# RWKV chunk matrices as 64x64 blocks, four heads to a stream, with the second stream half a round behind

## The reference

```python
def step(S, inp):
    rt, wt, kt, vt, kkt, at = inp
    sa = einsum('bhvk,bhk->bhv', S, -kkt)
    S = S * wt[:, :, None, :] + sa[..., None] * (kkt * at)[:, :, None, :] + vt[..., None] * kt[:, :, None, :]
    return S, einsum('bhvk,bhk->bhv', S, rt)
S1, y = lax.scan(step, S0, xs)      # 512 steps
```

## Time and profile before

| | |
|---|---|
| timed, median of 3 runs | 5242.58 us (5240.49 to 5243.71) |
| profiled execution | 5239.91 us, span 5238.2 us |
| TensorE busy | 91% of the span |
| VectorE / ScalarE / GpSimd busy | 55% / 30% / 26% |
| mean granted TensorE clock | 0.937 |

### The profile page before, as it was taken

One profiled execution on the slowest core, in us unless ns is written; L12 is line 12 of the kernel. 1 busy time (PEld: TensorE's weight loads), 2 busy tenths in 40 slices (PEclk: granted clock), 3 DMA queues, 4 the chain that ended last, 5 costly groups with the idle time before them and its releaser, 6 DMA issues. The chain is left out here.

```text
span 5238.2 us, 59995 instructions
## 1 busy us (share of the span) xinstructions
PE 4753.3 (91%) x23383; PEld 3839.2 (73%) x23383; DVE 2866.4 (55%) x4356; ACT 1594.0 (30%) x3108; POOL 1339.3 (26%) x571
## 2 busy tenths in 40 slices
PE   8996649699999999999997987789999999999997
PEld 5665328577888887788886655577788787788886
DVE  1044455424987862566663016813977872566665
ACT  1020202112456662222222012311366563222222
POOL 0000000001443444444441000001433444444442
PEclk9995759899999999999998996889999999999999
DMA  4232100022566685555552231132566676455552
GB/s 148 81 105 68 36 17 1 34 87 87 160 178 174 194 237 173 188 194 194 194 193 77 94 97 49 37 105 75 155 178 183 176 220 207 163 193 193 194 193 91
DMA packets 531708, 709.99 MB, mean 136 GB/s; under 512 B 47625, under 2 KB 415874, under 8 KB 510434
## 3 DMA queue, kind: packets, MB, share of 16 engines
q1 hardware_dynamic: 526004, 689.08, 40.8%
q0 software_dynamic: 4608, 16.78, 1.0%
q10 hardware_dynamic: 814, 0.29, 0.0%
HBM read 552.62 MB, written 149.21 MB: 134 GB/s over the span
## 5 line engine op out<-in xcount | busy, mean ns | idle before, releaser
L2304 PE MATMUL ps<-h_parts,u_parts 128*128 128x512 f32 x6144 | 1431.1, 393 | 23.2 <-PEq L1803 13.3
L2555 PE MATMUL ps<-w_parts,v_parts 128*128 128x512 f32 x6144 | 1398.1, 390 | 14.8 <-DVE w_parts L2540 14.8
L2555 PEld LDWEIGHTS ps<-w_parts,v_parts 128*128 128x128 f32 x6144 | 1156.8, 188 | 256.0 <-POOL v_parts L2526 15.5
L2304 PEld LDWEIGHTS ps<-h_parts,u_parts 128*128 128x128 f32 x6144 | 1151.5, 189 | 260.6 <-POOL u_parts L1781 13.8
L1781 POOL TENSOR_TENSOR u_parts<-u_turned,u_parts 128x1024 fp32r<-128x1024 f32 x256 | 664.1, 2595 | 2065.0 <-ACT u_parts L1776 2064.9
L2540 DVE TENSOR_TENSOR w_parts<-w_rows,w_parts 128x512 fp32r<-128x512 f32 x256 | 625.1, 2442 | 481.5 <-ACT w_parts L2519 481.5
L211 PE MATMUL ps<-h,arena 128*128 128x264 f32 (+2 forms) x2176 | 486.3, 387 | 81.3 <-DMA arena<-in_even_w_out_dram 33.4
L2526 POOL TENSOR_TENSOR v_parts<-u_rows,v_parts 128x1024 fp32r<-128x1024 f32 x172 | 413.0, 2402 | 539.9 <-ACT v_parts L2517 539.9
L211 PEld LDWEIGHTS ps<-h,arena 128*128 128x128 f32 (+1 forms) x2176 | 411.6, 189 | 156.6 <-DMA arena<-in_even_w_out_dram 33.8
L2082 DVE TENSOR_TENSOR onehots<-iota,choice 128x1024 f32<-128x1024 f32 x256 | 385.6, 1546 | 189.4 <-PE ps L2336 187.8
L1768 DVE STREAM_TRANSPOSE u_turned<-u_rows 128x1024 f32<-128x1024 f32 x256 | 317.0, 1238 | 234.1 <-POOL u_parts L1781 212.4
(11 more groups left out here) (487 smaller groups left out, 4258.5 us busy)
## 6 DMA issues: line engine op xcount, KB each, us to landing
u_rows<-in_peer_u_dram SPq DMA_DIRECT2D x1024, 128.0 KB
u_rows<-in_peer_v_dram SPq DMA_DIRECT2D x86, 1024.0 KB, 4.7
hidden_tiles<-hidden SPq DMA_DIRECT2D x256, 256.0 KB
gate_matrices<-h SPq DMA_DIRECT2D x64, 1024.0 KB, 7.5
gates<-gate_matrices SPq DMA_DIRECT2D x32, 2048.0 KB, 7.9
u_turned<-hidden_tiles SPq DMA_DIRECT2D x256, 256.0 KB, 3.3
v_rows<-in_peer_v_dram SPq DMA_DIRECT2D x42, 1024.0 KB, 4.8
arena<-in_ada_w_dram SPq DMA_DIRECT2D x40, 1024.0 KB, 5.2
```

Of the source, the lines that this page charges most:

```text
L2304: ins = mm(ps[:, n % 2, :], q.uTs[:, n % 3, wp, k, :], q.hs[:, xp, k, :], start=k == 0 and (wp, xp) == (0, 0), stop=k == DT - 1 and wp == 1)
L2555: ins = nc.tensor.matmul(ps[:, o, :], q.vs[:, n % 3, vp, o * P:(o + 1) * P], q.ws[:, n % 3, wp], start=n == 0 and (vp, wp) == (0, 0), stop ...
```

## The change

The matrices are kept as the diagonal blocks alone: chunk 0 of a block in partitions 0 to 63, chunk 1 in partitions 64 to 127, both 64 columns wide. A stream now holds four heads (two tiles of heads) and a round is one block, so there are four rounds. Every product on chunk matrices becomes, for each head, two products of 64 rows, 64 output columns and 64 moving columns, on the two diagonal quarters of the array. Masks are kept 64 wide in a new buffer, `cmasks`, filled by two more copies in `rwkv_masks`. The transposes of R2 become ordinary products with the identity. The y copy moves from ScalarE to VectorE. L1 and L3 share buffers with M and X. CHAIN_LAG is 8: stream 1 is issued eight of sixteen steps behind stream 0.

```diff
+            v.tensor_copy(e.cmasks[0:64], m[0:64, :, 0:64])
+            link(v.tensor_copy(e.cmasks[64:P], m[64:P, :, 64:P]))
...
-CHAIN_PE, CHAIN_DVE, CHAIN_ACT = 22, 16, 10
-CHAIN_LAG = 0
+CHAIN_PE, CHAIN_DVE, CHAIN_ACT = 22, 16, 9
+CHAIN_LAG = 8
...
+    chunk_rows = (slice(0, 64), slice(64, P))
+    heads = [(i % 2, 64 * (i // 2)) for i in range(4)]
...
             def both(bank, lhs, rhs):
-                for i in range(2):
-                    ins = mm(ps[:, b + bank, i * P:(i + 1) * P], lhs[:, i, :], rhs[:, i, :], start=True, stop=True)
+                for i in range(4):
+                    for rows in chunk_rows:
+                        ins = mm(ps[rows, b + bank, i * 64:(i + 1) * 64], lhs[rows, i, :], rhs[rows, i, :],
+                                 start=True, stop=True)
                 ins.then_inc(made.sem, 1)
 
-            def inner(at, left, right):
-                for i, lo in enumerate(lows):
-                    ins = mm(ps[:, b + i, at:at + P], left[lo:lo + 64, tile, t], right[lo:lo + 64, tile, t],
-                             start=True, stop=True)
+            def inner(j, left, right):
+                for a in range(2):
+                    for c, rows in enumerate(chunk_rows):
+                        t = slice(t0 + 64 * c, t0 + 64 * c + 64)
+                        for side in range(2):
+                            at = j * P + a * 64
+                            ins = mm(ps[rows, b + side, at:at + 64], left[64 * side:64 * side + 64, 2 * x + a, t],
+                                     right[64 * side:64 * side + 64, 2 * x + a, t], start=True, stop=True)
                 return ins
 
             def turned(bank):
-                for i in range(2):
-                    ins = nc.tensor.transpose(ps[:, b + bank, i * P:(i + 1) * P], w.R2[:, i, :], s.ident[:])
+                for i in range(4):
+                    for rows in chunk_rows:
+                        ins = mm(ps[rows, b + bank, i * 64:(i + 1) * 64], w.R2[rows, i, :], s.ident[rows, rows],
+                                 start=True, stop=True)
                 ins.then_inc(made.sem, 1)
...
             dve_of(14)
-            for i, lo in enumerate(lows):
-                mm(ps[:, b + 1, i * P:i * P + 64], w.R2[:, i, :], w.tok[:, 0, lo:lo + 64], start=True, stop=True)
-                ins = mm(ps[:, b + 1, i * P + 64:(i + 1) * P], w.R2[:, i, :], w.LV[:, i, :], start=True, stop=True)
+            for i in range(4):
+                for rows in chunk_rows:
+                    mm(ps[rows, b + 1, i * P:i * P + 64], w.R2[rows, i, :], tok(0, i, rows), start=True, stop=True)
+                for rows in chunk_rows:
+                    ins = mm(ps[rows, b + 1, i * P + 64:(i + 1) * P], w.R2[rows, i, :], w.LV[rows, i, :],
+                             start=True, stop=True)
...
-            done(v.tensor_tensor(xb[:, tile, t], xb[:, tile, t], ps[:, b + 3, 0:P], ALU.add))
+            v.tensor_tensor(by_chunk(xb), by_chunk(xb), outs(0), ALU.add)
+            done(v.tensor_copy(by_chunk(e.y), outs(P)))
...
-            done(a.copy(w.tok, ps[:, b + 3, :].rearrange("p (j c) -> p j c", j=4)))
+            done(a.copy(w.tok.rearrange("p (g j) c -> p g (j c)", g=2), ps[:, b + 2:b + 4, :]))
...
-            done(a.copy(w.GU, w.bank(1)))
-            yield
-            pe_of(21)
-            done(a.copy(e.y[:, tile, t], ps[:, b + 2, 0:P]))
+            done(a.copy(w.GU, ps[:, b + 1, :].rearrange("p (i t) -> p i t", i=4)))
...
-        for step in range(8 * 16 + CHAIN_LAG):
+        for step in range(TT * 16 + CHAIN_LAG):
```

More of the change, by code:

```diff
@@ L1343, in products @@
         made, dve_did, act_did = s.chain_pe[x], s.chain_dve[x], s.chain_act[x]
[L1344 to L1347, removed]
+        tok = lambda j, i, rows: w.tok[rows, j, heads[i][0] * P + heads[i][1]:heads[i][0] * P + heads[i][1] + 64]
+        for blk in range(TT):
+            t0 = blk * P
+            dve_of = lambda n: pe.wait_ge(dve_did.sem, dve_did.at(CHAIN_DVE * blk + n))
+            act_of = lambda n: pe.wait_ge(act_did.sem, act_did.at(CHAIN_ACT * blk + n))
@@ L1366, in products @@
                 act_of(0)
+                dve_of(0)
             for j, src in enumerate((e.kt, e.ke, e.be, xb[:, 8:12, :])):
-                ins = nc.tensor.transpose(ps[:, b + 3, j * P:(j + 1) * P], src[:, tile, t], s.ident[:])
+                for a in range(2):
+                    at = (j % 2) * 256 + a * P
+                    ins = nc.tensor.transpose(ps[:, b + 2 + j // 2, at:at + P], src[:, 2 * x + a, t0:t0 + P], s.ident[:])
             ins.then_inc(made.sem, 1)
             yield
-            if quad:
-                dve_of(0)
@@ L1382, in products @@
             inner(0, e.bh, xb)
-            inner(P, e.kh, e.kt).then_inc(made.sem, 1)
+            inner(1, e.kh, e.kt).then_inc(made.sem, 1)
             yield
@@ L1403, in products @@
             both(1, w.M8, w.R)
-            for i, lo in enumerate(lows):
-                ins = mm(ps[:, b + 2, i * 64:(i + 1) * 64], w.L1[:, i, :], w.tok[:, 3, lo:lo + 64], start=True, stop=True)
+            for i in range(4):
+                for rows in chunk_rows:
+                    ins = mm(ps[rows, b + 2, i * 64:(i + 1) * 64], w.L1[rows, i, :], tok(3, i, rows), start=True, stop=True)
             ins.then_inc(made.sem, 1)
@@ L1430, in products @@
             act_of(8)
[L1431 to L1434, removed]
+            for i, (a, lo) in enumerate(heads):
+                for c, rows in enumerate(chunk_rows):
+                    moved, out = (ps[lo:lo + 64, b + 2 + c, at + a * 64:at + a * 64 + 64] for at in (0, P))
+                    mm(moved, w.GU[rows, i, 0:64], w.L3[rows, i, :], start=True, stop=True)
+                    mm(out, tok(3, i, rows), w.L2[rows, i, :], start=True, stop=False)
+                    ins = mm(out, w.GU[rows, i, 64:P], w.L3[rows, i, :], start=False, stop=True)
             ins.then_inc(made.sem, 1)
             yield
-            act_of(9)
             dve_of(15)
[L1439 to L1446, removed]
+            for i, (a, lo) in enumerate(heads):
+                for c, rows in enumerate(chunk_rows):
+                    step, add = (ps[lo:lo + 64, b + c + k, a * 64:(a + 1) * 64] for k in (0, 2))
+                    mm(step, w.GU[rows, i, 0:64], tok(2, i, rows), start=True, stop=True)
+                    mm(add, tok(1, i, rows), tok(3, i, rows), start=True, stop=False)
+                    ins = mm(add, tok(2, i, rows), w.GU[rows, i, 64:P], start=False, stop=True)
             ins.then_inc(made.sem, 1)
@@ L1454, in sums @@
         made, did = s.chain_pe[x], s.chain_dve[x]
[L1455 to L1460, removed]
-            done = lambda ins: ins.then_inc(did.sem, 1)
-            s.dve_chain.link(dve, v.tensor_tensor(
-                e.AT[:, tile, chunk:chunk + 2, :], e.id64[:].unsqueeze(1).to_broadcast([P, 2, 64]),
-                e.PL[:, tile, chunk:chunk + 2].unsqueeze(2).to_broadcast([P, 2, 64]), ALU.mult))
+        pair = lambda buf: buf.rearrange("p (l a) t -> p l (a t)", l=2)
+        masked = lambda dst, j, m: v.tensor_tensor(
+            dst.rearrange("p (l a) t -> p l a t", l=2),
+            ps[:, b:b + 2, j * P:(j + 1) * P].rearrange("p l (a t) -> p l a t", a=2),
+            e.cmasks[:, m, :].unsqueeze(1).unsqueeze(1).to_broadcast([P, 2, 2, 64]), ALU.mult)
+        outs = lambda at: ps[:, b + 2:b + 4, at:at + P].rearrange("p c (a t) -> p c a t", a=2)
+        for blk in range(TT):
+            tl, t, chunks = place(x, blk)
+            pe_of = lambda n: dve.wait_ge(made.sem, made.at(CHAIN_PE * blk + n))
+            own = lambda n: dve.wait_ge(did.sem, did.at(CHAIN_DVE * blk + n))
+            done = lambda ins: ins.then_inc(did.sem, 1)
+            by_chunk = lambda buf: buf[:, tl, t].rearrange("p a (c t) -> p c a t", c=2)
+            ins = v.tensor_tensor(e.AT[:, tl, chunks, :],
+                                  e.id64[:].unsqueeze(1).unsqueeze(1).to_broadcast([P, 2, 2, 64]),
+                                  e.PL[:, tl, chunks].unsqueeze(3).to_broadcast([P, 2, 2, 64]), ALU.mult)
+            s.dve_chain.link(dve, ins)
             yield
@@ L1514, in sums @@
             pe_of(21)
-            done(v.tensor_tensor(xb[:, tile, t], xb[:, tile, t], ps[:, b + 3, 0:P], ALU.add))
+            v.tensor_tensor(by_chunk(xb), by_chunk(xb), outs(0), ALU.add)
+            done(v.tensor_copy(by_chunk(e.y), outs(P)))
             yield
             pe_of(22)
-            v.tensor_tensor(e.AT[:, tile, chunk, :], e.AT[:, tile, chunk, :], ps[:, b, 0:64], ALU.add)
-            done(v.tensor_tensor(e.AT[:, tile, chunk + 1, :], e.AT[:, tile, chunk + 1, :], ps[:, b + 2, 0:64], ALU.add))
+            at = e.AT[:, tl, chunks, :].rearrange("p a c k -> p c a k")
+            done(v.tensor_tensor(at, at, ps[:, b:b + 2, 0:P].rearrange("p c (a k) -> p c a k", a=2), ALU.add))
             yield
@@ L1526, in copies @@
         made, did = s.chain_pe[x], s.chain_act[x]
-        for quad in range(8):
```

(25 more changed lines are left out.)

35 lines of the change are left out of this document (17 added, 18 removed).

## The result

| | before | after |
|---|---|---|
| timed, median | 5241.53 us (5238.39 to 5243.71, 4 runs) | 5177.2 us (5171.83 to 5178.52, 4 runs) |
| ratio | | 0.9876, 95% interval 0.9859 to 0.9893 |
| span of the profiled execution | 5238.2 us | 5176.2 us |
| chunk stage | 199.8 us | 135.2 us |

The kernel became 64 us faster (5241.5 less 5177.2; by the interval 56 to 74), and the stage alone lost 64.6: within the interval, all of it lies where the change was made. (The spans of the two profiled executions differ by 62.0; the other 2.6 us stand outside the stage, and runs of one kernel differ by more.) 5184 was forecast, with 142 for the stage. A stage is read here from its first transpose to the end of its last VectorE operation, to within 0.1 us.

The account below looks back on a forecast made before the run. TensorE was taken to bound the chunk stage, with VectorE late at one place. The stage was 115.5 + 9.3 + 3.5 + 13.4 = 141.7 us against 200.2, 58 off, giving 5184 us; range 5163 to 5210.

Parts of the forecast that it names:

- What one small product costs: Chunk stage: a 64 x 64 product with 64 moving columns takes 0.0295 us, bounds 0.027 and 0.055.
- Rival B: One PSUM bank serialises the two row tiles, 0.055 a record: stage 187 us, kernel 5229; chance 0.07 (with D).
- The inner products: Five inner product steps a stream-round: 16 records at 0.0295, 0.47 us each; 17.6 becomes 18.9 over the stage.
- The stalls: TensorE's waits in a double half-round: 1.7 us, plus 0.1 for restarting behind each of four waits.
- the changes of shape: Tile-shape changes remain only around the first transposes of a stream-round, 0.2 us on each side.
- The solve step and the y copy: TensorE waits at slots 5/13 and 7/15 of a half-round: 0.35 us and 0.75 us.
- The masks: Slot 1/9: four masks and the add delay TensorE 0.5 us, and the first stream's own step 0.1.
- The ends: Single-stream halves: first eight slots 9.3 us plus 3.5 at half clock, last eight 13.4.
- The offset: Streams half a round apart: the other stream's step stands in the 0.73 us gap; 64 steps become 72 slots.
- the two mask copies at nothing: Two added 384-column copies ahead, some 0.5 us each, hidden behind ScalarE's later end; without that cover 1 us.
- rival C: Clock stays low under quarter-array products, TensorE work x 1.8: stage 219 us, kernel 5262; chance 0.05.
- Rival A: VectorE later than laid out, or small products at 0.035 us: stage 162 us, kernel 5204; chance 0.14.

Follow-up runs that it names:

- experiment 6: Changed kernel with the loops of inner() ordered chunk first: 5169.66 us, 0.9870 of before, stage 135.5 us.
- Experiment 1: Changed kernel with CHAIN_LAG 0 for 8, blocks without the offset: 5152.53 us, 0.9841 of before, stage 117.3 us.
- experiment 2: Kernel before with CHAIN_LAG 8 for 0, the offset without blocks: 5265.09 us, 1.0050 of before, stage 222.7 us.
- experiment 4: CHAIN_LAG 16, second stream a whole round behind: kernel before 5260.38 us, stage 220.5; changed kernel 5172.85 us, stage 136.8.
- experiment 7: Changed kernel at CHAIN_LAG 0, last two steps ordered by kind of product across four quarters: 5149.15 us, 0.9834 of before, stage 111.1 us.
- experiment 8: Kernel of experiment 7 with the y copy back on ScalarE, moved r and y in separate banks: 5150.05 us; also with CHAIN_LAG 2: 5159.44 us.
- experiment 5: Changed kernel with the loops of both() turned, eight records in a row to one tile: 5182.43 us, stage 146.5 us.
- experiment 3: Changed kernel at CHAIN_LAG 0 plus four unused full-array transposes a stream-round among the small products: 5162.83 us, stage 125.3 us.

## Why the prediction was right

The time, the sign and the mechanism of the blocks held: the stage is bound by TensorE's issue, and the sum by records came within 6.5 us of 135.2. What did not hold is the reading of the offset, below.

- What one small product costs: 0.0295 taken, 0.029 measured in `both`. The two row tiles in one PSUM bank overlap, and 1536 records show it where eight groups of L1610 had to stand for it. By the rule of the Trainium skill, in TensorEngine Tiling (Array Packing), Gotcha 1: PSUM Pressure, the stage would have taken 187; for row tiles that write different partitions of the bank the traces here disagree with it. Rival B is out.
- The inner products, 0.47 a call, are the term that was mis-sized: 0.24 to 0.26. Their four products in a row go to four different quarters, and all four work at once; I had only pairs in view, since L1610, the row that I took the price from, uses two. 80 records x 0.0135 is 1.1 us a half-round less work; the half-round is 15.6 for 16.5. These 0.9 x 7 are 6.3 of the miss of 6.5. That it is this term follows from the row; experiment 6 was to prove it by taking it away, and didn't. The distances between starts bear it out: in the round from 811.58 to 842.71 those above the records' own pace hold 5.5 us in all, 2.8 a half-round, which leaves 12.8 for the records at their pace, where the sum had 14.0.
- The stalls: 2.1 a half-round forecast (and 0.4 for the changes of shape), against the 2.8 just read. The solve step and the y copy have their waits where 0.35 and 0.75 were forecast (0.29 and 0.38 above; the starts stand 0.5 and 0.6 apart there, since a row counts only the idle time behind the modelled end of the record before). The masks cost less than the 0.5 and 0.1 taken: idle time behind them is 0.17 (before 816.43) and 0.05 (before 832.52). One more, 0.44 behind ScalarE's copy of U in L1581, I had held to be covered. The sum is near by errors that cancel.
- The ends: 26.2 forecast for two single halves and the low clock; 135.2 - 7 x 15.6 is 26. The first eight slots took 12.8 (767.65 to 780.44), just the 9.3 + 3.5 of the forecast, though the clock came up in the stretch 776 to 779, later than the 773 of before. What offset this is most likely the same term: all five inner calls stand in these slots and cost 1.1 us less at full clock. No run shows it apart, so part of this agreement is luck.
- The offset: I priced its ends and let it "stand in the gap" of the other stream. That reading was wrong, though no number of the forecast hung on it. Experiment 1 shows the round 2.5 us longer than in step. For the blocks the difference is in TensorE's stops: the distances above the records' pace hold 5.5 us of a round with the offset and 3.2 in step. My reading, argued and not shown by a run, is that streams on the same step cover like with like, a 0.94 step behind a 0.94 step, while half a round apart 0.47 steps have to cover the waits of long ones. For the old form the cause is another: its round is 24.8, 26.6 and 24.8 at lags 0, 8 and 16, with 9, 19 and 9 changes of tile shape and no more idle time (experiments 2 and 4). The blocks' rounds are 28.65, 31.1 and 29.95, so for them unequal steps are a part and not all.
- The masks' cost, the two mask copies at nothing and rival C: as forecast. While TensorE ran 64x64 products, busy 111 us of 124, the granted clock was 1.00 from 779 on (0.96 over the whole stage). Rival A's 0.035 didn't come.

What stays nearly open: what the "issue" stops of experiments 4, 7 and 8 are. The trace's DMA records tell where they stand. In all runs shown, the stage has 25 such stops above 0.15 us (ten with lag 2, six and four in the other runs of 8 and 7, four with blocks at lag 16, one of 0.19 in run 1, none in the changed kernel and none in the old form). Each of the 25 ends 1.2 to 1.6 us after a packet of the queue that brings instructions has landed: in run 7 TensorE goes on at 818.23 and at 874.89, the packets before had landed at 816.92 and at 873.46. These packets, 16 KB each, come only every 3.9 us (28 in the 110 us of experiment 7, 8 in the same time of the kernel before), so this is not chance: TensorE very likely waits there for its own instructions. The number of packets alone doesn't bring the stops, since run 1 moved 26 in the same time with one short stop; run 7 issues the same records in less time. No run changed how instructions arrive, so it is read from the trace and not shown by an experiment.

## What to carry to other kernels

Count the records of small products by which part of the array each goes to: two in turn halve the price and four in turn quarter it (0.058, 0.029, 0.0145 us a record here). The loop order decides which you get, though TensorE looks some records ahead. When two changes come together, run each alone: here one gained 82 us and the other lost 18. Two streams on one in-order queue did best here on the same step, in both forms; before you set them apart, count how many changes of tile shape the new neighbours bring. And when records get very short, look for stops that nothing releases, and hold them against the landings of instruction packets.

## What was not expected of the hardware

- Products of 64 rows and columns in four quarters of the array run four at a time: 64 records in 1.16 us (827.15, experiment 1), also when eight records in a row go to only two of the quarters (0.016, experiment 6). With eight in a row to one quarter, two quarters overlap only in part (0.044, experiment 5).
- A full-array product between small ones costs 0.24 us beyond its own time, 0.12 for each change of tile shape (experiment 3); a change between full-array and 64 x 128 products costs 0.2 (experiment 2 and the earlier trace rows).
- When a 64x64 record starts every 0.0145 to 0.029 us, TensorE stops at times for 0.2 to 1.4 us, and each of these stops ends 1.2 to 1.6 us after an instruction packet has landed (25 of 25).
